# Idle transposes ahead of the first projection, its first chunk in order of arrival, and the side work of that projection moved one or two chunks later

## What is computed

```python
u = rms_norm(x, norm_mix[layer])
proj = u @ w_in
q, k, v, o, gates = jnp.split(proj, [QK_WIDTH, 2 * QK_WIDTH, 2 * QK_WIDTH + V_WIDTH, 2 * QK_WIDTH + 2 * V_WIDTH], axis=-1)
...
lf = jax.nn.log_sigmoid(gates[:, MLSTM_HEADS:])
```

## Time and profile before

| what | value |
|---|---|
| runs | 2548.05, 2547.39, 2544.04 us (median 2547.39) |
| profiled execution | 2546.21 us |
| its span, first to last instruction | 2544.5 us |
| TensorE busy | 2525.9 us, 99% of the span |
| VectorE, ScalarE, GpSimd busy | 1357.3, 984.0, 145.7 us |
| granted TensorE clock, mean | 0.996 of full |

### The profile page before, as it was taken

The page is one execution under the profiler, slowest core; times in us unless marked ns, Lnnn a source line. Parts: engine busy times, 40 slices in busy tenths (PEclk is TensorE's granted clock), DMA queues, the critical chain, the costliest instruction groups (busy, mean ns, idle before and its releaser), DMA issues. The chain is left out here.

```text
span 2544.5 us, 43299 instructions
## 1 busy us (share of the span) xinstructions
PE 2525.9 (99%) x16673; PEld 2465.0 (97%) x16673; DVE 1357.3 (53%) x2150; ACT 984.0 (39%) x1319; POOL 145.7 (6%) x313
## 2 busy tenths in 40 slices
PE   9999999999999999999999999999999999999998
PEld 8989898989999999999999999999999999999998
DVE  6464554547555544545545655764554555545554
ACT  5333333234433333433323444543333333333444
POOL 1100000002030000000000011300000000000001
PEclk9999999999999999999999999999999999999999
DMA  6547373635544444444444453444444444444443
GB/s 174 190 133 248 117 259 113 234 125 178 163 145 138 150 143 142 144 147 142 142 145 145 131 181 103 140 159 155 150 149 152 150 150 142 157 152 150 137 158 106
DMA packets 227568, 390.50 MB, mean 153 GB/s; under 512 B 25736, under 2 KB 55808, under 8 KB 227056
## 3 DMA queue, kind: packets, MB, share of 16 engines
q1 hardware_dynamic: 215444, 368.10, 45.7%
q10 hardware_dynamic: 11928, 19.73, 2.1%
HBM read 364.76 MB, written 23.43 MB: 153 GB/s over the span
## 5 line engine op out<-in xcount | busy, mean ns | idle before, releaser
L1282 DVE TENSOR_TENSOR w_lo<-w_raw,w_hi 128x1024 fp32r<-128x1024 f32 x664 | 813.5, 1230 | 1054.6 <-ACT w_hi L922 1054.1
L922 ACT ACTIVATE w_hi<-w_raw 128x1024 fp32r<-128x1024 f32 x664 | 699.2, 1058 | 1331.2 <-PE bank L487 1314.5
L485 PE MATMUL bank<-xh,w_hi 128*128 128x336 f32 (+2 forms) x3584 | 1133.4, 316 | 4.1 <-DVE xl L1291 3.6
L486 PE MATMUL bank<-xl,w_hi 128*128 128x336 f32 (+2 forms) x3584 | 1126.3, 314 | 0.0
L487 PE MATMUL bank<-xh,w_lo 128*128 128x336 f32 (+2 forms) x3584 | 1124.5, 314 | 0.0
L485 PEld LDWEIGHTS bank<-xh,w_hi 128*128 128x128 f32 x3584 | 674.1, 188 | 21.9 <-issue 18.4
L486 PEld LDWEIGHTS bank<-xl,w_hi 128*128 128x128 f32 x3584 | 675.1, 188 | 1.1 <-issue 1.0
L487 PEld LDWEIGHTS bank<-xh,w_lo 128*128 128x128 f32 x3584 | 675.8, 189 | 0.0
L485 PE MATMUL bank<-hh,w_hi 128*128 128x336 f32 (+1 forms) x1632 | 511.2, 313 | 0.5 <-DVE w_lo L1282 0.5
L486 PE MATMUL bank<-hl,w_hi 128*128 128x336 f32 (+1 forms) x1632 | 509.2, 312 | 0.0
L487 PE MATMUL bank<-hh,w_lo 128*128 128x336 f32 (+1 forms) x1632 | 509.1, 312 | 0.0
(11 more groups left out here) (293 smaller groups left out, 967.7 us busy)
## 6 DMA issues: line engine op xcount, KB each, us to landing
w_raw<-in_w_up SPq DMA_DIRECT2D x640, 256.0 KB, 2.8
w_raw<-in_w_down SPq DMA_DIRECT2D x336, 256.0 KB, 3.4
w_raw<-in_w_mlstm_in SPq DMA_DIRECT2D x192, 256.0 KB, 3.4
area<-in_state_mlstm_C SPq DMA_DIRECT2D x32, 512.0 KB, 8.4
w_raw<-in_w_mlstm_out SPq DMA_DIRECT2D x64, 256.0 KB, 3.3
out_C_sample<-area ACTq DMA_DIRECT2D x32, 512.0 KB, 6.2
w_raw<-in_w_up SPq DMA_DIRECT2D x64, 192.0 KB, 2.5
w_raw<-in_w_pool SPq DMA_DIRECT2D x16, 256.0 KB, 2.8
```

What stands on the lines that cost most here:

```text
L485: pe.matmul(out, wh, xhk, start=first, stop=False)
L486: pe.matmul(out, wh, xlk, start=False, stop=False)
L922: nc.scalar.activation(w_hi[:, s], w_raw[:, s], ACT.Copy).then_inc(hi_done, 1)
L1282: V.tensor_tensor(w_lo[:, s], w_raw[:, s], w_hi[:, s].bitcast(F32), ALU.subtract).then_inc(lo_done, 1)
```

## The change

Only TensorE's list changes. (1) After turn 0 it issues FILL = 28 more transposes of the identity. (2) c0 gets a function of its own, `first_chunk`: it waits for the high part of x and the low part of the weights, runs the 16 matmuls that need no low x over all four banks, then waits for low x and runs the other 8. (3) Turn 2 moves from ahead of c2 to ahead of c3, turn 3 from ahead of c4 to ahead of c5, `gates` from ahead of c5 to ahead of c6, and `row_scales` from ahead of c6 to ahead of c7, directly before `parameters`.

```diff
+FILL = 28
...
+            def first_chunk(banks, c):
+
+                pe.wait_ge(lo_done, c + 1)
+                pe.wait_ge(xh_done, 2)
+                for t in range(4):
+                    for w in (w_hi, w_lo):
+                        for j in range(2):
+                            pe.matmul(banks[t][:, 0:T], w[:, 0, j, t * P:t * P + P], xh[:, j, :],
+                                      start=w is w_hi and j == 0, stop=False)
+                pe.wait_ge(xl_done, 2)
+                for t in range(4):
+                    for j in range(2):
+                        mm_ = pe.matmul(banks[t][:, 0:T], w_hi[:, 0, j, t * P:t * P + P], xl[:, j, :], start=False, stop=False)
+                mm_.then_inc(chunk_used, 1)
...
-                for i in range((nkt + 1) // 2):
+                for i in range(done, (nkt + 1) // 2):
...
             to_features(0)
+            for _ in range(FILL):
+                pe.transpose(SA[0][:, 0:P], ident[:, :], ident[:, :])
...
                 if first:
-                    gemm(SA, c, 0, KT, 4, xh, xl, 0, fresh=lambda kt: pe.wait_ge(xl_done, kt + 2),
-                         amid={1: lambda: to_features(1), 2: lambda: to_features(2), 4: lambda: to_features(3), 5: gates,
-                               6: row_scales, 7: parameters})
+                    first_chunk(SA, c)
+                    gemm(SA, c, 0, KT, 4, xh, xl, 0, done=1, fresh=lambda kt: pe.wait_ge(xl_done, kt + 2),
+                         amid={1: lambda: to_features(1), 3: lambda: to_features(2), 5: lambda: to_features(3), 6: gates,
+                               7: scales_and_parameters})
```

More of the change, by code:

```diff
@@ L487, in split_products, with gemm @@
                 return pe.matmul(out, wl, xhk, start=False, stop=last)
-            def gemm(banks, c, k0, nkt, nt, xhi, xlo, c0, free=None, guard=None, fresh=None, amid=None):
-                for i in range((nkt + 1) // 2):
+            def first_chunk(banks, c):
[11 more added lines that the diff above has]
+                mm_.then_inc(chunk_used, 1)
+            def gemm(banks, c, k0, nkt, nt, xhi, xlo, c0, free=None, guard=None, fresh=None, amid=None, done=0):
+                for i in range(done, (nkt + 1) // 2):
                     if amid and i in amid:
@@ L571, in parameters, with scales_and_parameters @@
                 m_.then_inc(st_tr, 1)
+            def scales_and_parameters():
+                row_scales()
+                parameters()
             pe.wait_ge(consts, 1)
```

## The result

| | before | changed |
|---|---|---|
| median | 2545.28 us (7 runs, 2544.04 to 2548.05) | 2554.44 us (7 runs, 2551.88 to 2555.78) |
| profiled execution | 2546.21 us | 2552.63 us |
| its span | 2544.5 us | 2550.9 us |

The table ahead of the prediction had the first three of the seven runs of before, with a median of 2547.39 us. The changed kernel is slower: the ratio is 1.0031, interval 1.0021 to 1.0040, or 9.2 us between the medians. In a later session with its own runs of both kernels (experiment 11) it was 1.0027, 1.0016 to 1.0038, or 6.85 us.

A forecast was written before the change was run, and what follows sets the result against it. TensorE was taken as the bound, keeping to the end what it gains or loses at the start. +3.1 us at one clock plus +1.6 for one clock fall gave +4.7, or 2552.1 us from the median; range 2547.2 to 2556.0.

The forecast's parts named there:

- The head start: At c0: the 28 transposes fill idle time and keep the clock full, so turn 1 starts 2.98 us ahead.
- the place of low x: Inside c0: reordering the same 24 matmuls around low x adds nothing, since the transposes end after what they would wait for.
- The wait at c3: After turn 2: TensorE waits 1.95 us for VectorE's low part of c3, queued behind the copies after that turn.
- The wait at c6: After the gates: TensorE waits 2.3 us for c6's low part, which hangs on turn 3; c6 begins at 44.2.
- The wait at `columns`: Ahead of `columns`: TensorE waits 2.0 us for evictions behind VectorE's 13.86 us gate-row chain, which hangs on the scales.
- Sum at one clock: At `columns`: head start and the three waits together, less overlap with slack, make it +3.1 us late, 63.3 against 60.19.
- The clock: In the three waits: one fall taken, a cold stretch of 3.4 us costing +1.6 us; ends 0 and +4.8; chance 0.35.
- The price per cold us: From c0 against c3 at full clock: each cold us of work costs 0.46 us.
- the rival with two or three falls: Clock falls in two or three of the three waits: +6.3 to +7.9 us, 2553.7 to 2555.3; chance 0.24.
- the 28 don't hold the clock: Rival at c0: it starts cold at 11.67, the 2.98 us are gone, all waits stay: +6.1, 2553.5; chance 0.05.
- the waits don't form: Rival at c3 and c6: low parts come in time, TensorE keeps its 2.98 us: 2544.4; chance 0.08 including only one wait.
- the clock holds in all waits: Rival: no fall of the clock in any of the three waits: +3.1 us, 2550.5; chance 0.28.

The follow-up runs named there:

- experiment 11: The changed kernel once more, unaltered, in a later session beside its own runs of the kernel before: 2553.01 us beside 2546.16, ratio 1.0027.
- experiment 1: Changed kernel with the old places of the side work put back; the 28 transposes and `first_chunk` stay: 2548.10 us, ratio 1.0007 to before.
- 8: Changed kernel with c3 and c4 ahead of turn 2's copies, c6 ahead of squares and their sum, `columns` ahead of c11, GpSimd's clearing later: 2545.89 us, ratio 1.0002.
- 10: Changed kernel with c3, c6 earlier, c4 between turn 2's copies and scalings, `columns` ahead of c11, GpSimd's clearing later: 2544.91 us, ratio 0.9995 to before.
- 2: Kernel before with only the new places of the side work, without the 28 transposes and with c0 as before: 2557.38 us, ratio 1.0045.
- experiment 3: Changed kernel with VectorE's low part of c3 put ahead of the copies after turn 2: 2553.94 us, ratio 1.0032 to before.
- 4: Changed kernel with c3's low part ahead of turn 2's copies, and c6 ahead of the squares and their sum: 2550.24 us, ratio 1.0018 to before.
- experiment 5: Changed kernel with GpSimd's two clearings held until VectorE has the absolute gate rows: 2551.27 us, ratio 1.0022 to before.
- experiment 7: Changed kernel without the 28 transposes (FILL = 0): 2556.25 us, ratio 1.0041 to before.
- experiment 9: Changed kernel with c3, c6 earlier, c4 between turn 2's copies and scalings, GpSimd's clearing later, `columns` still ahead of c10: 2546.68 us, ratio 1.0003 to before.

## Why the prediction was right or wrong

Forecast were 2552.1 us, 4.7 more than before; measured were 2554.44, and 9.2 more (6.85 in the later session). Each wait stands where the prediction put it and for the reason it gave; two sizes were too small.

*The head start*: right, 3.17 us at turn 1 for 2.98 forecast; 0.22 of it is an earlier turn 0 in that execution (7.08 for 7.30). That the place of low x adds nothing is wrong: in the changed kernel low x is done at 12.06 and c0 starts at 11.45, so the old order would have held c0 some 0.6 us longer (an estimate; no run has the 28 with the old order). That TensorE keeps to the end what it gains at the start is not borne out: in experiment 1 the lead ends at a load, in 8 at evictions, and 10 keeps part of it up to pooling.

*The wait at c3*: right in place and cause (1.79 for 1.95); experiments 2 and 3 show it. I had not seen what stood behind it: c4's low part is late too.

*The wait at c6*: right (2.12 for 2.3, c6 at 44.0 for 44.2); experiments 2 and 4 show it.

*The wait at `columns`*: right in place and cause, mis-sized: 2.82 for 2.0. I took the 13.86 us of VectorE's chain over from the kernel before; it took 63.95 - 49.39 = 14.56, since moving the scales next to the parameters also moved GpSimd's clearing onto the chain. Experiment 5 shows that this is worth 1.0 us. I had followed SyncE's queue past the moved step, and not GpSimd's.

*Sum at one clock*: +3.9 at `columns` for +3.1.

*The clock*: one fall in three waits was right in the profiled executions of the changed kernel (two of two), but its price was 3.1 us and not 1.6. The term that was mis-sized is the length of the stretch: I took the 3.4 us of pooling's, and this one lasted 6.8, as the one at the start had: from 10.63 (0.57 in 10.60 to 10.80), 1.95 us after turn 0 had ended at 8.68, to 17.44 or 17.45 (0.86 in 17.40 to 17.60), where the 5.21 cold us of c0 end. Behind `columns` it was 6.8 in every run in which the clock fell there but experiment 3 (3.4); behind c3 it was 3.4 (experiments 2 and 7), in pooling 3.4 or 6.8. What decides between the two is open. The price per cold us, 0.46, was right (3.1 / 6.8). The kernel before bears it out too: c0's matmuls start 0.28 us apart up to 17.41, at 0.50 of the full clock, and c3's 24 take 3.73 / 24 = 0.155 each at 1.00, which gives 1 - 0.155 / 0.28 = 0.45.

With the two terms as measured the sum for the profiled execution is 3.9 + 3.1 = 7.0, and 6.4 came out. The median of 2554.44 lies in the range, but on the side of 0.2% that I gave 0.40, and with some luck: the forecast was counted from 2547.39, the median of three runs, and all seven have 2545.28. As a difference I forecast +4.7, with a range from -0.2 to +8.6; 9.2 lies just outside it, 6.85 inside. The two mis-sized terms explain the 6.85, not the rest of the 9.2. The time is that of the rival with two or three falls (2553.7 to 2555.3), but the two profiled executions show one fall, twice as long. Of the other rivals, "the 28 don't hold the clock" is refuted by experiment 7 (0.50 in c0 without them, 1.00 with them), "the waits don't form" by the timeline, "the clock holds in all waits" by the windows. How many falls the runs without a profile had can't be seen; their times, from 2551.88 at a mean clock of 0.998 to 2555.78 at 0.995, go with the clock.

## What to carry to other kernels

A lead on the bounding engine is worth only what the next wait leaves of it: before moving side work to where the lead lets it fit, follow each thing that it releases through the other engines' lists to the next chunk's operands. Side work that is moved back by a chunk takes its whole chain with it, and what stood one chunk away is suddenly the bound; taking one such wait out (experiment 3) shows the next. Follow every engine's queue past a moved step, the idle one too: GpSimd did 1.8 us of work between c1 and `columns`, and did it in the wrong place. And a cold stretch is priced by its length, which was 3.4 or 6.8 us here at one and the same place: take both as ends.

## What was not expected of the hardware

A clearing by GpSimd of 1.20 us made an operation of 0.39 us on VectorE take 1.24; with the clearing later it took 0.38 (experiment 5). And the clock's answer to waits of about 2 us varied: it held through 1.79, 2.12 and 2.42 us (changed kernel, experiment 1) and fell behind 1.80 (experiments 2 and 7), 1.81 (experiment 5), 1.94 (experiment 9) and 2.82. In 2 and 7 it fell 1.1 and 1.3 us after the wait had ended, in 3 (2.82) 2.3 us after.
